# The output gate of the second recurrence, computed where its projection is evacuated

## What is computed

```python
def odd_layer(x, ...):
    ...
    r = (xr @ w_r); k = (xk @ w_k); v = (xv @ w_v)
    g = (xg @ w_g).astype(f32)
    ...
    o = wkv7_scan(r, decay, k, v, kk, a)        # state kept over the tokens
    ...                                         # group norm over each head
    bonus = jnp.sum(r * k * r_k, axis=-1, keepdims=True) * v
    o = (o + bonus.reshape(B_, S, D)) * jax.nn.silu(g)
    return o.astype(x.dtype) @ w_o
```

## Time and profile before

| | us |
|---|---|
| median of three runs | 3473.46 |
| lowest and highest | 3468.95 to 3474.69 |
| span of the profiled execution | 3469.8 |

### The profile page before, as it was taken

The page is one execution under the profiler, slowest core; times in us unless marked ns, Lnnn a source line. Parts: engine busy times, 40 slices in busy tenths (PEclk is TensorE's granted clock), DMA queues, the critical chain, the costliest instruction groups (busy, mean ns, idle before and its releaser), DMA issues.

```text
span 3469.8 us, 51688 instructions
## 1 busy us (share of the span) xinstructions
PE 3343.5 (96%) x21008; PEld 2676.9 (77%) x21008; DVE 1830.0 (53%) x2390; ACT 1416.6 (41%) x1624; POOL 405.8 (12%) x718
## 2 busy tenths in 40 slices
PE   7899999999999999999999999999999989999897
PEld 1578888888887888888887867888888867777685
DVE  5756666666667333444423457242424237777545
ACT  1334444444434233444423236141414157777423
POOL 0001232332112000000000000000000024444000
PEclk9999999999999999999999999999999999999998
DMA  9522222333223432222222313333333333333322
GB/s 354 183 76 89 103 94 89 110 107 109 100 94 103 154 133 96 82 87 75 86 88 91 134 62 135 120 120 120 121 120 121 134 96 88 77 84 67 127 97 73
DMA packets 178957, 381.46 MB, mean 110 GB/s; under 512 B 111729, under 2 KB 117105, under 8 KB 145009
## 3 DMA queue, kind: packets, MB, share of 16 engines
q1 hardware_dynamic: 164352, 326.73, 28.4%
q0 software_dynamic: 14448, 52.50, 4.5%
HBM read 342.49 MB, written 35.13 MB: 109 GB/s over the span
## 4 chain that ended last, share of the span: by engine, by line
PE 86%; DVE 4%; DMA 3%; POOLq 3%; SPq 2%; issue 2%; ACT 1%; DVEq 0%; POOL 0%; ACTq 0%
PE PJ L294 18%; PE PJ L296 18%; PE PJ L295 18%; PE AB L294 6%; PE AB L296 6%; PE AB L295 6%; POOLq L1619 1%; POOLq L1616 1%; PE AB L233 1%; DMA WK<-ada 1%; DMA X<-blocks_scratch 1%; PE AB L1723 1%; PE AB L1714 1%; PE AB L447 1%; PE AB L500 1%
## 5 line engine op out<-in xcount | busy, mean ns | idle before, releaser
L294 PE MATMUL PJ<-XH,WH 128*128 128x512 f32 x2848 | 1124.2, 395 | 17.2 <-DVE XL L421 10.3
L296 PE MATMUL PJ<-XH,WL 128*128 128x512 f32 x2848 | 1111.0, 390 | 0.0
L295 PE MATMUL PJ<-XL,WH 128*128 128x512 f32 x2848 | 1110.3, 390 | 0.0
L325 DVE TENSOR_TENSOR WL<-RAW,WH 128x2048 fp32r<-128x2048 f32 (+2 forms) x239 | 544.7, 2279 | 682.7 <-ACT WH L320 678.7
L320 ACT ACTIVATE WH<-RAW 128x2048 fp32r<-128x2048 f32 (+2 forms) x240 | 453.6, 1890 | 886.1 <-PE PJ L296 627.8
L294 PEld LDWEIGHTS PJ<-XH,WH 128*128 128x128 f32 x2848 | 535.9, 188 | 129.2 <-issue 17.1
L296 PEld LDWEIGHTS PJ<-XH,WL 128*128 128x128 f32 x2848 | 535.4, 188 | 112.7
L295 PEld LDWEIGHTS PJ<-XL,WH 128*128 128x128 f32 x2848 | 536.1, 188 | 109.8 <-issue 2.2
L294 PE MATMUL AB<-XH,WH 128*128 128x512 f32 (+1 forms) x960 | 380.4, 396 | 9.3 <-DVE XL L421 7.7
L296 PE MATMUL AB<-XH,WL 128*128 128x512 f32 (+1 forms) x960 | 374.8, 390 | 0.0
L295 PE MATMUL AB<-XL,WH 128*128 128x512 f32 (+1 forms) x960 | 374.7, 390 | 0.0
(11 more groups left out here) (462 smaller groups left out, 3911.1 us busy)
## 6 DMA issues: line engine op xcount, KB each, us to landing
RAW<-w SPq DMA_DIRECT2D x232, 1024.0 KB, 4.9
WK<-ada SPq DMA_DIRECT2D x32, 1024.0 KB, 5.8
GATE<-gate POOLq DMA_DIRECT2D x64, 256.0 KB, 3.0
rkvg_scratch<-WK POOLq DMA_DIRECT2D x16, 1024.0 KB, 4.7
x_scratch<-X POOLq DMA_DIRECT2D x8, 1024.0 KB, 5.7
X<-rkvg_scratch SPq DMA_DIRECT2D x32, 256.0 KB, 3.6
RAW<-rkvg_scratch SPq DMA_DIRECT2D x32, 256.0 KB, 3.4
X<-xT SPq DMA_DIRECT2D x4, 1024.0 KB, 15.5
```

What stands on the lines that cost most here:

```text
L294: nc.tensor.matmul(bank[0:width, n, :], hi, xh, start=first, stop=False)
L295: nc.tensor.matmul(bank[0:width, n, :], hi, xl, start=False, stop=False)
L296: m = nc.tensor.matmul(bank[0:width, n, :], lo, xh, start=False, stop=last)
L325: nc.vector.tensor_tensor(WL[k % 2][:, :, 0:w], narrow(RAW[k % 2], w), WH[k % 2][:, :, 0:w].bitcast(F32), ALU.subtract).then_inc(wl_ready, 1)
```

## The change

The gate's groups are evacuated by ScalarE alone, with Silu in place of the copy, in two instructions. What POOL stores in HBM is then silu(g). act_gate and dve_gate are gone, and so is the tile T_SG. sp_load brings three tiles, and a new sp_load_gate brings the fourth straight to T_GS, two iterations later, once the pair that had the tile two turns before has its result. It adds to the same `in0`/`in1`. sp_load waits for all earlier increments of its parity. dve_result waits for the gate's load.

```diff
+        def gate_act(act, n, bank):
+            def f():
+                act.wait_ge(s("rk_stored"), 16 * n)
+                act.wait_ge(evac_d, G_RW + n)
+                nc.scalar.activation(blocks4(wk(0, 2)), bank[:, 0:2, :], ACT.Silu).then_inc(evac_a, 1)
+                nc.scalar.activation(blocks4(wk(2, 2)), bank[:, 2:4, :], ACT.Silu).then_inc(evac_d, 1)
+            return f
...
         def sp_load(sp, q):
             if q == 4:
                 sp.wait_ge(s("rk_stored"), 256)
-            wait(sp, wv("gs"), q - 1)
+            wait(sp, wv(f"in{q % 2}"), 64 * (q // 2))
             wait(sp, wv("bv"), q - 1)
-            for m in range(4):
+            for m in range(3):
                 sp.dma_start(ws(T_IN(q) + m), rkvg_d[m, q]).then_inc(wv(f"in{q % 2}"), 16)
+
+        def sp_load_gate(sp, q):
+            wait(sp, wv("done"), q - 2)
+            sp.dma_start(ws(kept(q) + T_GS), rkvg_d[3, q]).then_inc(wv(f"in{q % 2}"), 16)
...
             at(t + 2, lambda q: sp_levels(sp, q), 2)
+            at(t + 2, lambda q: sp_load_gate(sp, q), 2)
             at(t + 4, lambda q: sp_load(sp, q), 4)
...
         def act_key_square(act, q):
-            act.wait_ge(wv(f"in{q % 2}"), 64 * (q // 2 + 1))
+            act.wait_ge(wv(f"in{q % 2}"), 64 * (q // 2) + 48)
...
-        def act_gate(act, q):
-            A(ws(T_SG), ws(T_IN(q) + T_G), ACT.Sigmoid).then_inc(wv("keys"), 1)
...
-            at(t + 3, lambda p: act_gate(act, p), 1)
...
         def dve_result(dve, t):
+            dve.wait_ge(wv(f"in{t % 2}"), 64 * (t // 2 + 1))
             dve.drain()
             V(tile(WK, t), ws(T_O(t)), ws(kept(t) + T_GS), ALU.mult).then_inc(wv("done"), 1)
-
-        def dve_gate(dve, q):
-            dve.wait_ge(wv("keys"), gate_ready(q))
-            dve.drain()
-            V(ws(kept(q) + T_GS), src(q, T_G), ws(T_SG), ALU.mult).then_inc(wv("gs"), 1)
...
-            at(t + 2, lambda p: dve_gate(dve, p))
...
             sp_solved_back(sp, 0)
+            sp.wait_ge(slot_done, SLOTS * G_OUT3)
+            for q in range(2):
+                sp_load_gate(sp, q)
             sp_load(sp, 2)
...
             for g in range(4):
-                act_group(act, G_RW + 12 + g, rw_act(act, 12 + g, (PJ, AB)[g % 2]), last=g == 3,
+                act_group(act, G_RW + 12 + g, gate_act(act, 12 + g, (PJ, AB)[g % 2]), last=g == 3,
...
-                dve_group(dve, G_RW + 12 + g, rw_dve(dve, 12 + g, (PJ, AB)[g % 2]), last=g == 3,
+                dve_group(dve, G_RW + 12 + g, lambda: None, last=g == 3,
```

More of the change, by code:

```diff
@@ L1473, in build @@
             30, 32, 33, 34, 36, 38, 39, 40, 41, 42, 43, 44, 45, 46)
-        T_B, T_EN, T_KK, T_NORM, T_LOGW, T_O2, T_SOLVE, T_SG, T_EB = 52, 53, 54, 55, 56, 57, 60, 62, 63
+        T_B, T_EN, T_KK, T_NORM, T_LOGW, T_O2, T_SOLVE, T_EB = 52, 53, 54, 55, 56, 57, 60, 63
         T_BP, T_EBP, T_A, T_AKK, T_D, T_K2, T_E, T_BONUS = 68, 68, 69, 69, 69, 70, 70, T_LOGW
@@ L1480, in build @@
         T_IN = lambda q: 48 if q % 2 == 0 else 64
-        T_R, T_KEY, T_V, T_G = range(4)
+        T_R, T_KEY, T_V = range(3)
         YT = lambda v: ws(T_Y + v % 2)
@@ L1492, in build @@
         wv = lambda n: s("wv_" + n)
-        for name in ("in0", "in1", "lw_in0", "lw_in1", "kksq", "keys", "lora", "sig", "ss", "sums", "exps", "factors", "tok", "tok_sb", "gs",
+        for name in ("in0", "in1", "lw_in0", "lw_in1", "kksq", "keys", "lora", "sig", "ss", "sums", "exps", "factors", "tok", "tok_sb",
                      "nt", "nt_sb", "bt", "masked", "r1", "bonus", "bv", "n_out", "n_in", "levels", "solved", "y_zero", "zeroed",
@@ L1521, in key_logged @@
         def key_logged(q):
-            return (3, 6)[q] if q < 2 else 4 * q
+            return (2, 5)[q] if q < 2 else 3 * q + 1
         def key_ready(q):
-            return (4, 7)[q] if q < 2 else 4 * q + 3
-        def gate_ready(q):
-            return 2 if q == 0 else min(4 * q + 6, 4 * PAIRS)
+            return 3 * q + 3
         def sp_load(sp, q):
@@ L1945, in first_act @@
                 act_key(act, 0)
-                act_gate(act, 0)
             elif k == 1:
@@ L2268, in _ @@
                 wv_sp(sp, t)
-            sp.wait_ge(wv("gs"), PAIRS)
             sp.wait_ge(wv("bv"), PAIRS)
```

## The result

The changed kernel took 3506.3 us (median; 3501.99 to 3507.7) against 3471.2 us (3466.95 to 3474.69) for the kernel before in the same session: 1.0085 times as long, 95% interval 1.0071 to 1.0100. The profiled execution answers the earlier trace rows with 34.7 us more.

A forecast was written before the change was run, and what follows sets the result against it. Dependences, not a full engine, bound the pairs' loop at 25.1 us a pair. Groups 0, boundary and first load +1.3, twelve pairs +8.4, tail 0: +9.7 on 3473.46 gives 3483.2 us; range 3474 to 3503.

The forecast's parts named there:

- The mechanism: SP's queue in the pairs' loop: SP stands still until the gate load has landed, 2.8 to 3.4 us, once per pair.
- Circle A: Pairs' loop: level copies, SP's loads, key's square, sum, back to next copies; forecast 25.8 us, between 24.9 and 26.7.
- The fixed part: Pairs' loop, TensorE's stretch from the sum to the next level copies: 12.76 us.
- DMA landings: SP's loads in the pairs: 2.8 to 3.4 us for the gate, 3.3 to 3.9 for the third load.
- The first rival: Pairs' loop: the new wait is hidden by short landings, period as now; 0 to +6, say 3476 us; chance 0.27.
- What leaves the engines: Pairs' loop: gate product and Sigmoid go, table load moves; gain and loss cancel, dve_d 0.1 us later.
- The second rival: Pairs' loop: the freed engines decide, not SP, so the kernel is faster; 3468 us; chance 0.06.
- The gate's groups: Projection groups: Silu evacuations by ScalarE alone; three groups cost nothing, after the last TensorE goes on about 1.8 us later.
- The first load: Start of the pairs: two gate loads, first landing awaited, then three loads; 7.7 us against 6.4, +1.3, bounds 0 and 3.
- Rival 3: Pairs' loop: new waits lower TensorE's clock, twelve times 1.7 us on top, 3503.6; chance 0.15, shared with further solved_out delays.
- the forecast's own last sign: Pairs' loop in the profile after: the forecast falls if the granted clock drops inside the loop.
- solved_out behind SP's stop: SP's queue in the pairs: solved_out delayed beyond the forecast; no size given; shares the chance of 0.15 with rival 3.

## Why the prediction was right and wrong

- **The mechanism: right.** SP stops once a pair for the gate's landing. Its stop was put at 2.8 to 3.4 us; it is 3.0 and 3.5 in the pairs shown. Taken away, the loss is gone (0.999); put alone into the kernel before, it comes (1.0053).
- **Circle A: right.** In the pair from 2948.13 it is 3.96 us to the gate's issue, 3.00 for its landing, 5.26 from the first of the three loads to the square, 0.77 to the sum, 12.76 to the next copies, 25.75 in all. The fixed part is that of the earlier trace rows to the hundredth. Undisturbed periods are 25.77, forecast 25.8. Two terms were off and nearly cancel, which is luck: the gate's issue came 3.96 us behind the copies (4.24 to 4.82), and the square 5.26 behind the first load (4.3 to 4.9). Against the rows' 25.1 that had been called +0.7; but 25.1 held a fall of the clock of the kernel before, and undisturbed it was 24.87, so the direct cost is +0.9 a pair. Twelve pairs give 10.8, close to the 10.3 of the table and above the forecast's 8.4.
- **DMA landings: rows over page.** The trace's lone loads land in 3.0 and 3.5 us. The Trainium skill (DMA: Bandwidth & Descriptors, Anatomy of one DMA) gave an estimate of 2.6; by it circle A would have been shorter than the period. The page's formula is for DMAs that GpSimd issues, and these are issued by SP, so it was a wrong guide here without being refuted for its own case. The first rival, which was that outcome, falls: the squares wait in every pair.
- **What leaves the engines: right.** The order on ScalarE is as worked out: from the end of the transposes to the level copy it is 2.53 us, 2.16 before, so 0.37 later where 0.36 was forecast. VectorE's dve_d waits for the growth factor:

```profile
2971.86 0.60 ACT L1912 ACTIVATE WS<-PJ 128x512 f32<-128x512 f32 x1 [0.78 <-PE PJ L1652]
2972.47 1.28 ACT L1863 ACT_TABLE_LOAD   x1
2973.77 0.69 ACT L1863 ACTIVATE GATE<-PJ,COL 128x512 f32<-128x512 f32 x1
2974.35 0.59 ACT L1920 ACTIVATE WS<-AB 128x512 f32<-128x512 f32 x1
...
2980.87 0.69 DVE L2030 TENSOR_TENSOR GATE<-GATE,X 128x512 f32<-128x512 f32 x1 [0.71 <-ACT X L1899]
```

The Sigmoid starts 0.02 us behind the end of the table load. The drain of 1.38 us that the Trainium skill (ScalarE: Activation LUTs, What ACT_TABLE_LOAD costs) counts on top doesn't appear, as it didn't in the rows before. With the stop taken away, gain and loss cancel: 24.86 against 24.87. The second rival, that the freed engines decide, falls with it.

- **The gate's groups: right but for one table load.** One load of Silu's table ahead of the first group and one ahead of the last, two activations of 1.03 and 1.02 us behind 8.90 us of idle ScalarE, and no wait of TensorE in the first three:

```profile
2739.85 1.03 ACT L1426 ACTIVATE WK<-AB 128x1024 f32<-128x1024 f32 x1 [8.90 <-PE AB L296]
2740.77 1.02 ACT L1427 ACTIVATE WK<-AB 128x1024 f32<-128x1024 f32 x1
...
2836.67 1.28 ACT L1426 ACT_TABLE_LOAD   x1
2837.97 1.02 ACT L1426 ACTIVATE WK<-AB 128x1024 f32<-128x1024 f32 x1
2838.89 1.02 ACT L1427 ACTIVATE WK<-AB 128x1024 f32<-128x1024 f32 x1
```

```profile
2840.05 1.10 PE L1688 MATMUL AB<-X,WK 64*64 64x128 f32 x32 [3.14 <-ACT WK L1427]
```

That these groups cost nothing is also seen from their starts, 43.52 us apart in both kernels. The last group is the answer to the earlier trace rows: TensorE waits 3.14 us where it waited 1.41, and goes on 2.1 us later relative to the evacuation of the group before; forecast 1.8. The forecast left out that the table must change back behind this Silu: a load of 1.28 us at 2842.10 stands ahead of the growth factor L1899, where the kernel before had none. It isn't on the chain to the third pair's square, since that chain is as long as before in the kernel with the gate's load behind the others, which has the same load of the table (65.8 us against 66.1).

- **The first load: a term that was mis-sized.** Forecast +1.3, bounds 0 and 3; measured +4.1. The stop is 4.9 us, not 3.1, and the gate's loads are issued 0.8 us later:

```profile
2840.36 3.46 SPq L1598 DMA_DIRECT2D WS<-solved_scratch  x2
2843.86 1.18 SPq L1551 DMA_DIRECT2D WS<-rkvg_scratch  x2
2848.72 1.27 SPq L1547 DMA_DIRECT2D X<-rkvg_scratch  x3
```

```profile
WS<-rkvg_scratch SPq DMA_DIRECT2D x1, 256.0 KB, 4.8
```

The gate's first load lands 4.8 us after its issue, and the issue of the two copies ahead takes 3.46 us, 1.28 before. From the gate's first load to the square it is 9.75 us, forecast 7.7. POOL's store of the last group, 1 MB, now runs at the same time, since the evacuation ends later; that it is the cause is argued and was not tried. Without the stop the chain is 67.5 us in place of 70.2, and with the gate's loads also issued behind the three others it is 65.8, against 66.1 before. So the stop is some 2.7 us of it and the place in the queue the rest. The price of a landing had been taken from quiet stretches and used in a crowded one.

- **The clock: the step that failed.** Rival 3 said what happened, with a chance of 0.15. What speaks against it was one wait of 1.42 us without a fall. By the forecast's own last sign it falls, since the granted clock drops inside the loop. The forecast itself made waits of about 2 us in every pair, and the one wait of 1.70 us that the trace had was followed by a fall. One row for and one against is no reason for 0.15, least of all where the expected waits lie beyond the row that fell. In the changed kernel the five longest waits for the square in the twelve pairs, 2.35 to 3.27 us, are followed by periods at 0.83, 0.83, 0.84, 0.89 and, once, 1.00; of the three of 1.90 to 1.99 two are at 0.94; those of 1.50 to 1.74 are all at 1.00. In its second profile the order is looser: waits of 2.71, 2.94, 3.08 and 3.56 us stand in periods at 1.00. (The one of 3.27 lies behind the stretch of the waits' view above.) Its price too was off, both ways. The 1.7 us of the earlier trace rows is right for that one period (0.06 x 27.70 = 1.7), but it was the smallest: the seven periods of the kernel after lost 1.6 to 5.2 us each, 3.6 on the mean. And it had twelve falls, where there were seven, against two before. 12 x 1.7 = 20.4 meets the measured 20.1 only because these two errors cancel, by luck.
- **The sum.** The profile has 34.7 us where 9.7 were forecast. Of the 25.0 between them 20.1 are the clock, which the sum had at nothing, 1.9 the direct part in the pairs (10.3 against 8.4), 2.8 the first load (4.1 against 1.3), and 1.9 and -1.7 lie ahead of the start-up chain and behind the loop.
- **The range.** It ended at 3503 because rival 3 did, and it held no case in which rival 3 came together with a start at its upper end. The measured 3506.3 is 3.3 above; the ratio of 1.0085 on the 3473.46 of the forecast is 3503. The changed kernel's other median, 3494.79, lies inside, though there too the excess over the kernel before, 18.1 us, is above the forecast's +7 to +17.
- **solved_out behind SP's stop**, named in the prediction as a possible delay, isn't seen as a wait of TensorE in the loop. It wasn't tested by itself.

Open: why one wait is followed by a fall and another isn't, such as 2.34 us with and 3.56 us without in one profile. The runs show that the idle time is the cause, not what decides each case; the length of the wait alone does not.

## What to carry to other kernels

Before a load is added to a counter that another wait on the same queue uses, look at who now waits for its landing: a queue that only issues can stop for 3 us by the count alone, and a counter of its own made the whole loss go away. Where a loop is bound by dependences, price a new wait of TensorE twice, once as it stands and once for the clock behind it, which here was two thirds of the loop's loss in one profile and a third in another. And ask of work that leaves whether its time reaches the end of the circle: here the product's gain on VectorE met a table load that had moved, and the Sigmoid and the product together brought nothing that these runs can tell.

## What the runs showed of the hardware

- Behind a single wait of 2.82 us TensorE ran at 1.2 GHz for some 10 us and lost 5.1 us of work: more than the wait. The same pair without a fall takes 25.5 to 25.8 us, with it 31.2.
- Unused matmuls in the wait held the granted clock at 1.00 in all 24 pairs that had them, where 19 of 60 pairs without fell. In the profiles they gave back 15.8 us (three) and 21.1 us (two) of the changed kernel's fourteen periods of 383.7, since part of their 0.95 us each stood on the path; against that kernel's second measurement (1.0056) the times of 1.0061 and 1.0045 are no gain that can be told.
- Waits of 3.9 to 6.3 us in every pair gave 0.80 to 0.89 in every pair, and periods of 30 to 34 us for 487 matmuls that take 24.9 undisturbed.
- The length of one wait does not tell whether the clock falls: none of 28 waits of the square's sum below 1.90 us was in a period with a fall and 19 of 32 longer ones were, but one of 3.56 us was not. Elsewhere in the loop falls came with waits of 1.60 and 1.70 us for VectorE.
- How often the clock falls differs between executions of one kernel: 22 us between the shortest and the longest of the changed kernel, at mean granted clocks of 0.987 and 0.979. A profile of one execution can overstate or understate such a cost.
